# An MLP in two phases, with the down product by one level of Strassen's scheme and the operand sums on POOL

## The reference

```
x = x + hybrid_mixer(rmsnorm(x))            # dilated + forgetting attention
x = x + cross_attention(rmsnorm(x), mem)
def _sq_relu_mlp(h, w_up, w_down):          # w_up (1024, 4096), w_down (4096, 1024)
    a = jax.nn.relu(h @ w_up)
    return (a * a) @ w_down
x = x + _sq_relu_mlp(rmsnorm(x, g_mlp), w_up, w_down)
y = rmsnorm(x, g_final)
```

## Time and profile before

| | us |
|---|---|
| median of the runs | 1726.22 |
| span of the profiled execution | 1724.9 |
| PE busy | 1672.5 (97%) |
| DVE busy | 729.9 (42%) |
| ACT busy | 586.3 (34%) |
| POOL busy | 0.2 |
| mean granted TensorE clock | 0.993 of full speed |

### The profile page before, as it was taken

How to read it: one execution, slowest core, us unless ns; L and a number is a source line. 1 busy time by engine, 2 the same in 40 slices (tenths; PEclk the granted TensorE clock), 3 DMA queues, 4 the chain that set the end, 5 groups by cost and what they waited for, 6 DMA issues and landing times.

```text
span 1724.9 us, 22386 instructions
## 1 busy us (share of the span) xinstructions
PE 1672.5 (97%) x8592; PEld 1417.7 (82%) x8592; DVE 729.9 (42%) x1371; ACT 586.3 (34%) x1014; POOL 0.2 (0%) x4
## 2 busy tenths in 40 slices
PE   5999999999999799999999999999999999999997
PEld 4788888888888688898888888888888888888886
DVE  6444444444444544652343364342424242424235
ACT  5445545445455542430252242121313130303022
POOL 0000000000000000000000000000000000000000
PEclk9999999999999899999999999999999999999999
DMA  5001110011010331251102012120202020203012
GB/s 187 17 25 27 38 27 16 24 40 27 25 39 13 112 109 37 69 151 49 37 25 74 16 34 62 58 77 13 85 12 85 12 85 12 85 3 94 0 37 97
DMA packets 99972, 87.72 MB, mean 51 GB/s; under 512 B 3984, under 2 KB 87056, under 8 KB 99888
## 3 DMA queue, kind: packets, MB, share of 16 engines
q1 hardware_dynamic: 99904, 86.75, 16.3%
HBM read 82.41 MB, written 4.85 MB: 51 GB/s over the span
## 4 chain that ended last, share of the span: by engine, by line
PE 89%; DVE 4%; ACT 4%; issue 1%; DMA 1%; SPq 0%; DVEq 0%
PE psG L527 18%; PE psG L529 18%; PE psG L528 18%; PE psG L544 15%; PE psO L676 7%; PE psS L625 3%; PE psG L607 2%; PE psS L556 2%; PE psS L555 2%; PE psS L811 1%; PE psS L572 1%; ACT khh L930 1%; PE psG L831 1%; DVE act_lo L1141 1%; DVE w_lo L1141 1%
## 5 line engine op out<-in xcount | busy, mean ns | idle before, releaser
L527 PE MATMUL psG<-act_hi,w_hi 128*128 128x512 f32 x640 | 249.5, 390 | 0.0
L529 PE MATMUL psG<-act_hi,w_lo 128*128 128x512 f32 x640 | 249.0, 389 | 0.0
L528 PE MATMUL psG<-act_lo,w_hi 128*128 128x512 f32 x640 | 249.0, 389 | 0.0
L527 PE MATMUL psG<-w_hi,a_hi 128*128 128x512 f32 x512 | 200.1, 391 | 0.7
L528 PE MATMUL psG<-w_lo,a_hi 128*128 128x512 f32 x512 | 199.3, 389 | 0.0
L529 PE MATMUL psG<-w_hi,a_lo 128*128 128x512 f32 x512 | 199.2, 389 | 0.0
L1110 ACT ACTIVATE r_ff<-psG 128x512 f32<-128x512 f32 x64 | 38.3, 598 | 446.7 <-PE psG L529 446.7
L1141 DVE TENSOR_TENSOR w_lo<-raw,w_hi 128x1024 fp32r<-128x1024 f32 x126 | 154.0, 1224 | 64.7 <-ACT w_hi L965 41.4
L1477 DVE TENSOR_TENSOR X<-X,psG 128x512 f32<-128x512 f32 x128 | 87.9, 687 | 212.9 <-PE psG L529 212.9
L676 PEld LDWEIGHTS psO<-V,pT 128*128 128x128 f32 x1152 | 149.8, 195 | 18.5 <-ACT pT L978 6.4
L965 ACT ACTIVATE w_hi<-raw 128x1024 fp32r<-128x1024 f32 x104 | 108.7, 1049 | 140.2 <-PE psG L529 83.0
(11 more groups left out here) (148 smaller groups left out, 2396.7 us busy)
## 6 DMA issues: line engine op xcount, KB each, us to landing
raw<-in_w_up_dram SPq DMA_DIRECT2D x32, 512.0 KB, 4.0
raw<-in_w_down_dram SPq DMA_DIRECT2D x32, 512.0 KB, 3.3
raw<-in_w_in_dram SPq DMA_DIRECT2D x22, 512.0 KB, 4.0
X<-in_x_dram SPq DMA_DIRECT2D x8, 512.0 KB, 8.2
raw<-in_w_out_dram SPq DMA_DIRECT2D x8, 512.0 KB, 3.9
raw<-in_w_xk_dram SPq DMA_DIRECT2D x8, 512.0 KB, 3.7
raw<-in_w_xv_dram SPq DMA_DIRECT2D x8, 512.0 KB, 3.7
raw<-in_w_xq_dram SPq DMA_DIRECT2D x8, 512.0 KB, 3.7
```

The source lines that it names most:

```text
L527: nc.tensor.matmul(dst, sh, mh, start=(k == 0), stop=False)
L528: nc.tensor.matmul(dst, sh, ml, start=False, stop=False)
L529: mm = nc.tensor.matmul(dst, sl, mh, start=False, stop=(k == n - 1))
```

## The change

The MLP is now two phases. The up phase runs all eight groups of up tiles, one after the other, with two sets of four weight slots. ACT takes the relu into `r_ff` (now four buffers), DVE squares it, and POOL stores the 256 KB tile to a DRAM tensor `a_rows`. The split of the squares moves to the down phase.

The down phase takes the 4096 features as four groups (`DOWN_GROUPS`) of 1024. In a group the squares A (features x tokens) and the weights B (features x columns) are cut in quarters of 512x512: A11 is the first half of the features with the first half of the tokens, A12 the second half of the features with the first tokens, A21 and A22 the same for the last tokens, and likewise B. Eight quarter products would be needed; the Winograd form of Strassen's scheme makes the same with seven, called parts 0 to 6 here. The operands are A11, B11 (part 0); A12, B21 (1); the sums SA and SB (2, and 3 in a new state); SA and B22 (4); A11 minus A21 with B22 minus B12 (5); and A22 with SB (6). POOL makes the sums from the loaded quarters, by eight subtractions or additions of 128x2048 elements in place, called #1 to #8 here in their order. Each operand is split by ACT (high part, L1257 and L1259 of the new file) and DVE (low part, `op_lo_out`, L1627) into one of two operand buffers; a new split of the same tensor is made where a sum stands in two parts. `part_bank` gives the four tiles of a part four PSUM banks, and the next part the other four, so all eight banks are in use.

The result of a part goes to the quarters of X that `DOWN` lists. A partial sum that three quarters of X share is kept in the SBUF tile `shared`: part 0 sets it (ACT copies it from PSUM), parts 3 and 5 add to it (DVE), and POOL adds it to the quarters of X, by twelve additions of 128x512 (`share`) per group. SP loads the quarters of the next group, each 1 MB, as their buffers come free.

The core of the diff:

```diff
-    r_ff = at("r_ff", [P, 2, HALF], f32, 130)
-    a_hi = at("a_hi", [P, 4, T], f32r, 174)
-    a_lo = at("a_lo", [P, 4, T], f32r, 190)
-
-    f_hn = [at(f"f_hn{i}", [P, D], f32, 106 + 4 * i) for i in range(2)]
-    f_gain = at("f_gain", [P, D], f32, 114)
+    r_ff = at("r_ff", [P, 4, HALF], f32, 174)
...
+    A11, B11, A12, B21 = (quarter_at(name, f32, kb) for name, kb in (("qA11", 198), ("qB11", 182), ("qA12", 190), ("qB21", 122)))
+    A21, A22 = act_f[0][:, 0:4, early], act_f[0][:, 4:8, early]
+    B12, B22 = act_f[1][:, 0:4, early], act_f[1][:, 4:8, early]
+    SA, SB = act_f[0][:, 4:8, late], act_f[1][:, 4:8, late]
+    opA = [(quarter_at("opA0_hi", f32r, 134), quarter_at("opA0_lo", f32r, 142)), (act_hi[:, 0:4, late], act_lo[:, 0:4, late])]
+    opB = [(quarter_at(f"opB{i}_hi", f32r, kb), quarter_at(f"opB{i}_lo", f32r, kb + 8)) for i, kb in enumerate((106, 150))]
...
+        DOWN = (((0, 0),), ((0, 0),), ((1, 1), (0, 1)), (), ((0, 1),), (), ((1, 0),))
...
+        def part_bank(n, s):
+            low = (psS[0][:, 0:HALF], psS[0][:, HALF:T], psS[1][:, 0:HALF], psS[1][:, HALF:T])
+            high = (psG[0][:], psG[1][:], psO[:, 0, :], psO[:, 1, :])
+            return (low, high)[n % 2][s]
...
-                for i in range(8):
-                    if i < 4:
-                        raw_block(g * 8 + (C_MLP + i), i % 2, w_up_k[:, :, bass.ds(g * HALF + i * P, P)], cols)
-                    else:
-                        raw_block(g * 8 + (C_MLP + i), i % 2, w_down[bass.ds(g * HALF + (i - 4) * P, P), :], lambda r: r[:])
-
-            sp.wait_ge(tile_done, G_MLP + (GROUPS - 1) * MLP_TILES + 8)
+                for i in range(4):
+                    raw_block(g * 4 + (C_MLP + i), i % 2, w_up_k[:, :, bass.ds(g * HALF + i * P, P)], cols)
...
+            for g in range(1, DOWN_GROUPS):
+                n, c = 7 * (g - 1), 8 * (g - 1)
+                sp.wait_ge(op_done, n + 1)
+                sp.wait_ge(sums_made, c + 2)
+                w_quarter("B11", B11, g, 0, 0)
+                sp.wait_ge(op_done, n + 2)
+                sp.wait_ge(sums_made, c + 6)
+                a_quarter("A12", A12, g, 1, 0)
+                w_quarter("B21", B21, g, 1, 0)
+                sp.wait_ge(sums_made, c + 7)
+                a_quarter("A11", A11, g, 0, 0)
+                sp.wait_ge(op_done, n + 5)
+                sp.wait_ge(sums_made, c + 8)
+                w_quarter("B22", B22, g, 1, 1)
+                sp.wait_ge(op_done, n + 6)
+                a_quarter("A21", A21, g, 0, 1)
+                w_quarter("B12", B12, g, 0, 1)
+                sp.wait_ge(op_done, n + 7)
+                a_quarter("A22", A22, g, 1, 1)
...
+        @block.gpsimd
+        def _(pool):
+            with pool.Fori(0, GROUPS) as g:
+                for j in range(8):
+                    half, c = divmod(j, 4)
+                    pool.wait_ge(sq_out, g * 8 + (j + 1))
+                    pool.dma_start(a_rows[bass.ds(g * HALF + c * P, P), half * HALF:(half + 1) * HALF],
+                                   r_ff[:, c, :]).then_inc(a_stored[c], 16)
+            def share(i, j, s):
+                nc.gpsimd.tensor_tensor(x_part(i, j, s), x_part(i, j, s), shared[:, s, :], ALU.add).then_inc(shared_added, 1)
+            def combine(dst, a, b):
+                nc.gpsimd.tensor_tensor(dst, a, b, ALU.subtract).then_inc(sums_made, 1)
+            for g in range(DOWN_GROUPS):
+                n, loaded = 7 * g, 16 * (g + 1)
+                if g:
+                    pool.wait_ge(op_done, n - 2)
+                else:
+                    pool.wait_ge(tile_done, G_MLP + 8 * GROUPS)
+                pool.wait_ge(quarter_loaded["A21"], loaded)
+                pool.wait_ge(quarter_loaded["A22"], loaded)
+                nc.gpsimd.tensor_tensor(SA, A21, A22, ALU.add).then_inc(sums_made, 1)
+                if g:
+                    pool.wait_ge(op_done, n)
+                pool.wait_ge(quarter_loaded["B11"], loaded)
+                pool.wait_ge(quarter_loaded["B12"], loaded)
+                combine(SB, B12, B11)
+                pool.wait_ge(op_done, n + 3)
+                pool.wait_ge(quarter_loaded["A11"], loaded)
+                combine(SA, SA, A11)
+                pool.wait_ge(quarter_loaded["B22"], loaded)
+                combine(SB, B22, SB)
+                pool.wait_ge(op_done, n + 4)
+                combine(SA, A12, SA)
+                combine(SB, SB, B21)
+                combine(A21, A11, A21)
+                combine(B12, B22, B12)
+                for s in range(4):
+                    pool.wait_ge(part_out, 4 * (n + 4) + s + 1)
+                    share(0, 1, s)
+                for s in range(4):
+                    pool.wait_ge(part_out, 4 * (n + 5) + s + 1)
+                    share(1, 0, s)
+                    share(1, 1, s)
...
+            def down_part(n):
+                a_op, b_op = opA[n % 2], opB[n % 2]
+                pe.wait_ge(op_done, n + 1)
+                for s in range(4):
+                    if n >= 2:
+                        pe.wait_ge(part_out, 4 * (n - 2) + s + 1)
+                    elif n == 1 and s < 2:
+                        pe.wait_ge(up_out, 8 * GROUPS)
+                    tok = slice(s * P, (s + 1) * P)
+                    for k in range(4):
+                        for r, (a, b) in enumerate(((0, 0), (0, 1), (1, 0))):
+                            mm = nc.tensor.matmul(part_bank(n, s), a_op[a][:, k, tok], b_op[b][:, k, :],
+                                                  start=(k == 0 and r == 0), stop=(k == 3 and r == 2))
+                    mm.then_inc(part_done, 1)
...
+            def op_hi_out(n):
+                g, pos = divmod(n, 7)
+                loaded, sums = 16 * (g + 1), 8 * g
+                a, b = ((A11, B11), (A12, B21), (SA, SB), (SA, SB), (SA, B22), (A21, B12), (A22, SB))[pos]
+                a_made = ((quarter_loaded["A11"], loaded), (quarter_loaded["A12"], loaded), (sums_made, sums + 1), (sums_made, sums + 3),
+                          (sums_made, sums + 5), (sums_made, sums + 7), (quarter_loaded["A22"], loaded))[pos]
+                b_made = ((quarter_loaded["B11"], loaded), (quarter_loaded["B21"], loaded), (sums_made, sums + 2), (sums_made, sums + 4),
+                          (quarter_loaded["B22"], loaded), (sums_made, sums + 8), (sums_made, sums + 6))[pos]
+                if n >= 2:
+                    act.wait_ge(part_done, 4 * (n - 1))
+                else:
+                    act.wait_ge(tile_done, G_MLP + 8 * (GROUPS - 1 + n))
+                act.wait_ge(*a_made)
+                nc.scalar.activation(opA[n % 2][0], a, ACT.Copy).then_inc(op_hi, 1)
+                act.wait_ge(*b_made)
+                nc.scalar.activation(opB[n % 2][0], b, ACT.Copy).then_inc(op_hi, 1)
...
+            def op_lo_out(n, side):
+                hi, lo = (opA, opB)[side][n % 2]
+                pos = n % 7
+                src = ((A11, A12, SA, SA, SA, A21, A22), (B11, B21, SB, SB, B22, B12, SB))[side][pos]
+                dve.wait_ge(op_hi, 2 * n + side + 1)
+                e = nc.vector.tensor_tensor(lo, src, hi.bitcast(f32), ALU.subtract)
+                if side:
+                    e.then_inc(op_done, 1)
+            def part_add(n, s):
+                pos = n % 7
+                dve.wait_ge(part_done, 4 * n + s + 1)
+                g = n // 7
+                if pos == 0:
+                    dve.wait_ge(shared_set, 4 * g + s + 1)
+                if pos == 3:
+                    dve.wait_ge(part_out, 4 * (n - 3) + s + 1)
+                if pos == 5:
+                    dve.wait_ge(shared_added, shared_out(g, 0, 1, s))
+                if pos in (3, 5):
+                    e = nc.vector.tensor_tensor(shared[:, s, :], shared[:, s, :], part_bank(n, s), ALU.add)
+                for i, j in DOWN[pos]:
+                    if pos == 2 and g:
+                        dve.wait_ge(shared_added, shared_out(g - 1, i, j, s))
+                    if pos == 6:
+                        dve.wait_ge(shared_added, shared_out(g, i, j, s))
+                    before = max([m for m in range(n) if (i, j) in DOWN[m % 7]], default=None)
+                    if before is not None:
+                        dve.wait_ge(part_out, 4 * before + s + 1)
+                    src = shared[:, s, :] if pos == 0 else part_bank(n, s)
+                    e = nc.vector.tensor_tensor(x_part(i, j, s), x_part(i, j, s), src, ALU.subtract if pos == 6 else ALU.add)
+                e.then_inc(part_out, 1)
...
+            for n in range(N_PARTS):
+                if n + 1 < N_PARTS:
+                    op_lo_out(n + 1, 0)
+                part_add(n, 0)
+                if n + 1 < N_PARTS:
+                    op_lo_out(n + 1, 1)
+                for s in range(1, 4):
+                    if n == N_PARTS - 2:
+                        final_var(s - 1)
+                    part_add(n, s)
+                    if n == N_PARTS - 2:
+                        final_scale(s - 1)
```

(76 more changed lines are left out.)

118 lines of the change are left out of this document (68 added, 50 removed).

## The result

| | before | after |
|---|---|---|
| median of the runs, us | 1727.2 (four runs) | 1745.12 (1744.85 to 1746.28, four runs) |
| span of the profiled execution, us | 1724.9 | 1743.7 |
| mean granted TensorE clock | 0.993 | 0.977 |

What follows compares the result with a forecast made beforehand. PE, busy 97% of the span with 89% of the chain, was taken as the bound. 1724.9 - 43.5 - 3.0 + 0.8 + 50 = 1729.2 us of span, median 1730.5; range 1677 to 1757, the forecast's own 1718 to 1743.

Steps and rivals of the forecast that it cites:

- Matmuls removed: Down product on PE: 1344 matmuls in place of 1536, at an unchanged 226.7 ns each, 43.5 us less.
- The rival of slower laid-out code: Down phase: 1344 matmuls laid out one by one run slower than 226.7 ns; 1% would be 3 us; among others, 0.03.
- Boundaries: Up phase: the loss of 0.38 us at each of eight group boundaries goes, 3.0 us less.
- stores and loads at nothing: POOL's stores in the up phase and the quarter loads of 1 MB cost no time.
- Who disturbs whom: Down phase: DVE's low parts and POOL's sums take turns, one whole instruction at a time, as if sharing one reading port.
- Rival one: Down phase: no exclusion between DVE and POOL, or none DVE feels, so no stall; 1680.5 us; chance 0.22.
- POOL's price: POOL's sums of 2048 elements take 4.42 us and additions of 512 take 1.23, the upper values assumed.
- The walk: One steady down group: PE waits 4.2, 0.4, 7.0 us ahead of parts 1, 3, 4; 12.5 with hand-offs, 50 in four.
- rival two: Start of part 4: POOL keeps the port through a run of sums, 5.1 us more per group, 1751 us; chance 0.12.
- The tail: After the last matmul: DVE's norm chain in part 6 ends some 0.8 us later behind PE, 0.8 us more.
- The sum: All terms on the profiled span give 1729.2 us; the median lies 1.3 above, 1730.5 us.
- rivals one and three: Rival one has its line; three: softer coupling, DVE and POOL slowed while overlapping, part of the stalls, 1690 to 1720; chance 0.06.

Runs made afterwards that it cites:

- the run with fills: Changed kernel with each of POOL's sums replaced by two zero fills of the same 128x2048 tile, so POOL writes without reading; 1691.44 us, ratio 0.9797.

## Why the prediction was right or wrong

- **Matmuls removed (-43.5): right.** Without gaps 1344 matmuls take 304.6 us (all sums on DVE: 1366.39 to 1670.80, and one pace), and 28 x 10.88 is 304.6. The rival of slower laid-out code is excluded.
- **Boundaries (-3.0), stores and loads at nothing: right.** No wait of PE in the up phase; POOL's store of 256 KB lands in 2.4 us, median.
- **Who disturbs whom: right, and shown.** DVE and POOL take turns by whole instructions as supposed, and the run with fills shows that writing alone does not bring it about. Rival one (1680.5) is false: the exclusion is there. Its picture of the down phase without a stall is met where POOL's sums are gone; that run takes 1693.0 us, and most of the rest is the tail (8.2 more than was forecast) and the stages ahead of the MLP (3.7 there).
- **POOL's price: nearly right.** The upper end was taken, 4.42 us and 1.23; alone they take 4.6 (1391.36 in the first group) and 1.30. The upper end was called a guess, and it was a lucky one.
- **The walk: right in sum, wrong in its parts.** I gave 88.7 us per steady group with hand-offs (76.2 + 12.5), and #3 recurs after 88.76 (1391.36 to 1480.12). That the two agree so closely is in part luck: POOL's price was low by 0.18 us, which over seven sums on the chain makes 1.3 us, and 0.9 us of hand-offs was a guess. And I had it all as gaps. It is 2.6 and 6.0 of gaps and 1.7 and 2.2 of slow matmuls: **the step that failed is that matmuls keep the pace of the earlier trace rows behind a gap.** The slow matmuls of part 4 make PE 2.2 us later at part 1, so the gap there is 2.6 and not 4.2, and those of part 1 shorten the one ahead of part 4. In the steady groups this changes little, for a chain through POOL's sums sets the period and the slow matmuls take up part of the wait. In the first group both add up: gaps of 6.1 and 6.0 with 2.1 and 2.2 behind them, 16.5 us for my 12.5. Down phase in all: 54.2 us for my 50.
- **The first group** also has rival two's order, once: the low part for part 1 starts at 1368.99 and takes 11.50 us, until both #1 and #2 are done. Everywhere else DVE gets in after one. Why not there is open; POOL's last store (1368.53) and #1 (1369.17) lie on both sides of its start.
- **The tail (+0.8): wrong, +9.0.** This is the term that was sized worst, and **the second step that failed**: I counted DVE's norm chain in part 6 alone and with nothing in its way. (Even so, 3.2 us for each tile against 2.72 of PE make 1.4 over the three steps to the last tile, and not 0.8.) The eight additions of part 5 by POOL fall on the norm of tiles 0 to 3, and there even the one-column instructions with two SBUF operands wait for a whole POOL instruction, so that DVE enters the last part late (POOL's row, then DVE's within it):

```profile
1708.59 10.50 POOL L611 TENSOR_TENSOR X<-X,shared 128x512 f32<-128x512 f32 x6 [2.86 <-DVE shared L1642]
```

```profile
1716.21 0.41 DVE L1320 SCALAR_TENSOR_TENSOR newt<-rstd,var 128x1 f32<-128x1 f32 x1
1716.65 0.15 DVE L1322 TENSOR_SCALAR newt<-newt 128x1 f32<-128x1 f32 x1
1716.84 1.03 DVE L1324 TENSOR_TENSOR rstd<-rstd,newt 128x1 f32<-128x1 f32 x1
1717.90 2.27 DVE L1328 SCALAR_TENSOR_TENSOR f_hn<-X,rstd,f_gain 128x1024 f32<-128x1024 f32 x1
```

These took 0.22, 0.15, 0.16 and 1.28 us where POOL is silent (0.23, 0.17, 1.28 in the earlier trace rows). DVE makes its first addition of part 6 at 1727.23, 10.2 us after that tile's matmuls (1717.07). Without POOL's additions it comes 4.2 us after them and the tail is 12.3 us. So 6 us are waits for POOL. The other 3 us over the old 9.3 go with the norms of tiles 0 to 3, which lie beside the low parts in part 5 and make DVE late even then; no run took them apart.

- **The sum.** 1730.5 forecast and 1745.1 measured: 8.2 from the tail, 4.2 from the down phase, 2.1 from the stages before the MLP (open whether the change's), of 14.5 between the spans. The value lies just outside the forecast's own range (to 1743) and inside the whole range; the chances leaned by a hair to faster, and the case of rivals one and three had too much weight.

## What to carry to other kernels

Count the shared port like an engine: add up DVE's instructions with two SBUF operands and POOL's that read SBUF, by what each holds it. Here that was 34.6 + 52.4 = 87 us in a period of 76 us of PE. By this sum no order of the same instructions hides it, and the one other cut that was run, into quarters, was slower still. On DVE the same sums take half the port's time, and a DVE that is 93% busy cost PE nothing. A total that fits is not enough by itself: with six sums on DVE and two on POOL it fitted, and PE still waited 8 us. And a gap of PE can be charged twice, once as a wait and once in the clock behind it, so a gap that is moved is not a gap that is gone.

## What the runs showed of the hardware

- Gaps of PE of 2.6 us were followed by a stretch at the 1.2 GHz level each time, which cost 1.7 us over ten matmuls; behind gaps of 6.0 us it cost 2.2. The three gaps of 1.9 us, with six sums on DVE, had no such stretch behind them.
- A DVE instruction of one column with two SBUF operands waits for POOL's whole instruction as a large one does (0.16 us became 1.03).
- POOL's fills of 128x2048 take 1.81 us and run beside DVE's two-operand low parts, which keep their 2.29 us; its additions of the same size take 4.6.
- POOL's additions of 128x512 take 1.30 us, four of them in a row 5.0, which is more than one of 128x2048.
